# Prompt attention in another order of tiles, its keys and values loaded a stage ahead, and the last row's value pages on two queues

## The reference

```
z = rms_norm(h) @ w_in                      # q, k, v, gates of both groups, 3600 columns
q, k = rms_norm per head half               # 4 heads, two halves of 64 each
prompt:  s_m = q_m k_m^T / 8 + bias(n), causal, m = 0, 1;  p = softmax(s_0) - lam softmax(s_1);  o = p v
sample:  the same against 32 cached pages of each sequence (page_table) and its new tokens
group B: gated linear attention in chunks of 128, prompt and sample
h + concat(rms_norm(o) * gate_d, rms_norm(o_g) * gate_g) @ w_out
```

## Time and profile before

| | us |
|---|---|
| runs: median (lowest, highest) | 1161.14 (1158.05, 1163.96) |
| profiled execution, time | 1162.31 |
| its span | 1160.6 |
| TensorE busy | 1037.6 (89%) |
| VectorE busy | 545.6 (47%) |
| ScalarE busy | 468.1 (40%) |
| GpSimd busy | 234.5 (20%) |
| loads and stores | 200.34 MB, mean 173 GB/s |

### The profile page before, as it was taken

One profiled execution on the slowest core, in us unless ns is written; L12 is line 12 of the kernel. 1 busy time (PEld: TensorE's weight loads), 2 busy tenths in 40 slices (PEclk: granted clock), 3 DMA queues, 4 the chain that ended last, 5 costly groups with the idle time before them and its releaser, 6 DMA issues. The chain is left out here.

```text
span 1160.6 us, 26456 instructions
## 1 busy us (share of the span) xinstructions
PE 1037.6 (89%) x9067; PEld 837.1 (72%) x9067; DVE 545.6 (47%) x1376; ACT 468.1 (40%) x1353; POOL 234.5 (20%) x385
## 2 busy tenths in 40 slices
PE   4999999999999999989899899767686899889978
PEld 4899999977677776656577667546565788778755
DVE  4755533334434332242343434546746766566421
ACT  5732322344443322333323344426646645545330
POOL 0000100013222222120222323339830111011100
PEclk9999999999999999999999999987895799999989
DMA  7322655569898687575799877657223122211101
GB/s 194 121 89 68 203 164 180 147 210 328 288 312 283 228 274 232 191 217 192 246 287 304 306 252 245 209 157 233 72 60 106 49 95 73 73 58 37 54 24 43
DMA packets 111575, 200.34 MB, mean 173 GB/s; under 512 B 15402, under 2 KB 51444, under 8 KB 111444
## 3 DMA queue, kind: packets, MB, share of 16 engines
q1 hardware_dynamic: 75892, 118.22, 33.1%
q0 software_dynamic: 20480, 67.13, 17.1%
q10 hardware_dynamic: 15072, 13.31, 3.4%
HBM read 179.79 MB, written 19.60 MB: 172 GB/s over the span
## 5 line engine op out<-in xcount | busy, mean ns | idle before, releaser
L1149 PE MATMUL bank<-ww,xTh 128*128 128x256 f32 (+1 forms) x1728 | 333.4, 289 | 11.9 <-DVE qwr L1357 9.8
L1149 PEld LDWEIGHTS bank<-ww,xTh 128*128 128x128 f32 (+1 forms) x1728 | 272.6, 188 | 20.4 <-DVE qwr L1357 11.6
L259 POOL DMA_DIRECT2D vraw<-in_cache_v x256 | 138.0, 539 | 622.5 <-issue 620.1
L1149 PE MATMUL bank<-ww,xTl 128*128 128x256 f32 (+1 forms) x864 | 246.0, 285 | 0.0
L477 DVE COPY kt<-bank 128x512 f32<-128x512 f32 x128 | 88.6, 692 | 183.5 <-PE bank L280 119.7
L1149 PEld LDWEIGHTS bank<-ww,xTl 128*128 128x128 f32 (+1 forms) x864 | 162.3, 188 | 0.0
L280 PE MATMUL bank<-ident,kraw 128*128 128x128 f32 x1024 | 153.3, 279 | 0.4 <-DVE kt L477 0.3
L401 ACT ACTIVATE kt<-bank 128x512 f32<-128x512 f32 x128 | 76.2, 595 | 159.6 <-PE bank L280 159.0
L280 PEld LDWEIGHTS bank<-ident,kraw 128*128 128x128 f32 x1024 | 112.8, 141 | 22.5 <-issue 21.6
L302 PE MATMUL bank<-kt,qq 128*32 128x128 f32 x2048 | 81.2, 278 | 17.0 <-DVE kt L477 16.2
L2322 ACT ACTIVATE e<-bank,sm 128x128 f32<-128x128 f32 (+8 forms) x66 | 49.6, 752 | 84.0 <-DVE sm L2433 84.0
(11 more groups left out here) (253 smaller groups left out, 1598.4 us busy)
## 6 DMA issues: line engine op xcount, KB each, us to landing
vraw<-in_cache_v POOLq DMA_DIRECT2D x256, 256.0 KB, 4.6
kraw<-in_cache_k SPq DMA_DIRECT2D x256, 256.0 KB, 4.1
wraw<-in_w_in SPq DMA_DIRECT2D x28, 512.0 KB, 5.2
out<-nat ACTq DMA_DIRECT2D x32, 128.0 KB, 2.0
wo_raw<-in_w_out SPq DMA_DIRECT2D x8, 512.0 KB, 8.8
xr<-in_x_prompt SPq DMA_DIRECT2D x7, 512.0 KB, 3.4
out<-xr SPq DMA_DIRECT2D x7, 512.0 KB, 2.6
bT<-in_x_prompt SPq DMA_DIRECT2D x4, 512.0 KB, 4.2
```

The source lines that it names most:

```text
L259: pool.dma_start(vraw[:, p % VR, :], cache_v.rearrange("a n p h d -> (a n) p (h d)")[bass.ds(page, 1)] .rearrange("o p c -> (o p) c")).the ...
L1149: ins = pe.matmul(z_at(u)[0:r, 0:CB], a[:, k, P * i:P * i + r], b[:, wslot(c), k, :], start=(n == 0), stop=(n == 3 * KT - 1))
```

## The change

The attention stage takes the tiles in the order 3, 7, 6, 5, 4, 2, 1, 0, 8 (order, place); what hung on a tile's number in buffers, semaphores and fills now hangs on its place. Keys are no longer turned one tile ahead: keys 0 to 3 are turned before the first unit, keys 4 to 8 in the first three units of tile 3. For this all key rows are loaded in the linear attention stage, into keys_raw, which lies over w_out's raw blocks 3 to 7; these five blocks are loaded only when the last key is turned, and weights_hi(3) waits for all five. Value rows 0 to 6 are loaded at the end of the linear attention stage, rows 7 and 8 at the start of the attention stage. On ScalarE and VectorE the split of the bias band, and VectorE's wait for the norm weights, stand ahead of the first query and key halves. In the sample attention the odd value pages of the last row are issued by SyncE (by_sp). The meta tokens' rows of the residual are loaded, where a buffer was set to zero before.

```diff
+        KEPT = 3
+        FIRST = 3
+        keys_raw = Area(nc, WOL + 4 * KEPT * D, WOL + 4 * KT * D).take("keys_raw", [P, TILES, W])
+        VD = SB_HIGH - 4 * TILES * W
+        vd = Area(nc, VD, SB_HIGH).take("vd", [P, TILES, W])
...
+        def by_sp(p):
+            return p >= NP - NPAGES and p % 2 == 1
+        def value_in(p):
+            first = NP - NPAGES
+            if by_sp(p):
+                return v_last[p // GRP % 2], 16 * GRP // 2 * ((p - first) // VR + 1)
+            return v_in[p % VR], 16 * (p // VR + 1)
...
+                        if b is not None and t >= 1 and by_sp(b * NPAGES + (t - 1) * GRP + n):
+                            load_value(sp, b * NPAGES + (t - 1) * GRP + n)
...
-                for k in range(KT):
+                for k in range(KEPT):
                     sp.dma_start(wo_raw[:, k, :], w_out[0, k * P:(k + 1) * P, :]).then_inc(wo_in, 16)
...
+                sp.dma_start(first_q[:], q_d[FIRST]).then_inc(first_in, 16)
+                for i in range(TILES):
+                    n = min(P, L - P * i)
+                    sp.dma_start(keys_raw[0:n, i, :],
+                                 k_prompt.rearrange("a b l h d -> (a b l) (h d)")[P * i:P * i + n, :])\
+                      .then_inc(keys_in, 16)
...
+                for i in range(LT_ - 1):
+                    sp.dma_start(vd[:, i, :], v_prompt.rearrange("a b l h d -> (a b l) (h d)")[P * i:P * i + P, :])\
+                      .then_inc(vd_in, 16)
...
-            units = [(i, h) for i in range(TILES - 1) for h in range(H)] + [(TILES - 1, H - 1)]
+            order = [FIRST] + [i for i in range(TILES - 2, -1, -1) if i != FIRST] + [TILES - 1]
+            place = {i: t for t, i in enumerate(order)}
+            units = [(i, h) for i in order[:-1] for h in range(H)] + [(TILES - 1, H - 1)]
...
-                return [[("k", i + 1)], [("q", i + 1, 0)], [("m", i - 1)] if i >= 1 else [], [("q", i + 1, 1)]][h]
+                t, h = place[units[u][0]], units[u][1]
+                x = [[], [("q", order[t + 1], 0)], [("m", order[t - 1])] if t >= 1 else [], [("q", order[t + 1], 1)]][h]
+                if t == 0:
+                    x = x + [[("k", 4), ("k", 5)], [("k", 6)], [("k", 7), ("k", 8)], []][h]
+                return x
+            first_turns = [("q", order[0], 0), ("q", order[0], 1)] + [("k", i) for i in range(FIRST + 1)]
...
+                sp.wait_ge(turned_done, turn_no[("k", TILES - 1)] + 1)
+                sp.wait_ge(wo_in, 16 * KEPT)
+                for k in range(KEPT, KT):
+                    sp.dma_start(wo_raw[:, k, :], w_out[0, k * P:(k + 1) * P, :]).then_inc(wo_in, 16)
...
-                    back = 2 if small(u) else 1
+                    back = 2 if small(u) and small(u - 1) else 1
...
                 def weights_hi(k):
                     if k == 0:
+                        act.wait_ge(wo_in, 16 * KEPT)
+                        act.wait_ge(dw_scaled, 1)
+                    if k == KEPT:
                         act.wait_ge(wo_in, 16 * KT)
-                        act.wait_ge(dw_scaled, 1)
...
-                queries_lo(0, 0)
-                keys_lo(0)
-                queries_lo(0, 1)
                 dve.wait_ge(dw_in, 32)
...
+                for x in first_turns:
+                    if x[0] == "q":
+                        queries_lo(x[1], x[2])
+                    else:
+                        keys_lo(x[1])
```

More of the change, by code:

```diff
@@ L186, in hymba_kernel @@
         v_in = [sem(f"v_in{n}") for n in range(VR)]
-        c_in = sem("c_in")
+        v_last = [sem(f"v_last{n}") for n in range(2)]
         vn_in = sem("vn_in")
@@ L228, in advancer, with load_value @@
             return go
+        def by_sp(p):
[5 more added lines that the diff above has]
+            return v_in[p % VR], 16 * (p // VR + 1)
+        def load_value(eng, p):
+            if p >= VR:
+                b, g = (p - VR) // NPAGES, (p - VR) % NPAGES // GRP
+                eng.wait_ge(pv_done, b * RG + g + 2)
+            page = eng.value_load(pages[0:1, p:p + 1], min_val=0, max_val=POOL - 1)
+            eng.dma_start(vraw[:, p % VR, :],
+                          cache_v.rearrange("a n p h d -> (a n) p (h d)")[bass.ds(page, 1)]
+                          .rearrange("o p c -> (o p) c")).then_inc(value_in(p)[0], 16)
         def decode_sp(sp):
@@ L1880, in hymba_kernel @@
             mix = m_.take("mix_b", [P, W])
+            xr = m_.take("xr", [P, D])
             r4 = m_.take("r4", [P, 3, 4])
@@ L1889, in hymba_kernel @@
             pO = bank[:, 5, :]
-            vd_in = [sem(f"vd_in{n}") for n in range(2)]
             qk_in = [sem(f"qk_in{n}") for n in range(2)]
@@ L1966, in extras @@
                     return []
-                i, h = units[u]
-                return [[("k", i + 1)], [("q", i + 1, 0)], [("m", i - 1)] if i >= 1 else [], [("q", i + 1, 1)]][h]
-            turns = [("q", 0, 0), ("k", 0), ("q", 0, 1)]
+                t, h = place[units[u][0]], units[u][1]
[4 more added lines that the diff above has]
+            first_turns = [("q", order[0], 0), ("q", order[0], 1)] + [("k", i) for i in range(FIRST + 1)]
+            turns = list(first_turns)
             for u in range(NU + 1):
@@ L1990, in wait_bank @@
                     if turns[n][0] == "q":
-                        eng.wait_ge(qlo_done, 2 * turns[n][1] + turns[n][2] + 1)
+                        eng.wait_ge(qlo_done, 2 * place[turns[n][1]] + turns[n][2] + 1)
                     if turns[n][0] == "k":
@@ new lines, in _ @@
+                sp.wait_ge(g_out, 96)
+                load_x(order[0], xr_in)
+                for t in range(1, TILES):
+                    if t >= 2:
+                        sp.wait_ge(mix_done, t - 1)
+                        load_gate(order[t - 1])
+                    if t + 1 < TILES:
+                        if t >= 2:
+                            sp.wait_ge(turned_done, turn_no[("q", order[t - 1], 1)] + 1)
+                        load_q(order[t + 1])
+                    if t >= 3:
+                        store_y(order[t - 3])
+                        sp.wait_ge(y_out, 16 * (t - 2))
+                        load_x(order[t - 2], xr_in)
@@ L2098, in _ @@
+                sp.wait_ge(turned_done, turn_no[("q", order[LT - 1], 1)] + 1)
+                load_x(order[LT], xr8_in)
                 sp.wait_ge(scores_done, 2 * NU)
-                load_x(LT - 1, xr7_in)
+                load_x(order[LT - 1], xr7_in)
                 sp.wait_ge(mix_done, LT)
-                load_gate(LT)
-                for i in range(LT - 2, TILES):
-                    store_y(i)
+                load_gate(order[LT])
+                for t in range(LT - 2, TILES):
+                    store_y(order[t])
@@ L2221, in turn_mix @@
                     r = rows_of(i)
-                    pe.wait_ge(mix_done, i + 1)
+                    pe.wait_ge(mix_done, place[i] + 1)
                     wait_bank(pe, ("m", i))
@@ L2249, in project, with fill @@
                         ins.then_inc(d_free, 1)
-                def fill(u, place):
-                    for i, j in fills.get((u, place), []):
+                def fill(u, at):
+                    for i, j in fills.get((u, at), []):
                         project(i, j)
-                prepare(("q", 0, 0))
-                prepare(("k", 0))
-                prepare(("q", 0, 1))
+                for x in first_turns:
+                    prepare(x)
                 pe.wait_ge(bandhi_done, 2)
@@ L2278, in _ @@
                         scores(u, 1)
-                turn_mix(TILES - 2)
-                for place in range(2):
-                    fill(NU + 1, place)
+                turn_mix(order[-2])
+                for at in range(2):
+                    fill(NU + 1, at)
                 for j in range(8):
-                    project(LT - 1, j)
-                turn_mix(TILES - 1)
+                    project(order[-2], j)
+                turn_mix(order[-1])
                 for j in range(8):
-                    project(LT, j)
+                    project(order[-1], j)
             @block.scalar
@@ L2441, in combine @@
                     dve.wait_ge(exp_done, 2 * u + 2)
-                    if begins(u) and i >= 2:
-                        dve.wait_ge(out_copied, i - 1)
-                    dve.reciprocal(inv[:, i % 2, h:h + 1], s[:, 2:3])
+                    t = place[i]
+                    if begins(u) and t >= 2:
+                        dve.wait_ge(out_copied, t - 1)
+                    dve.reciprocal(inv[:, t % 2, h:h + 1], s[:, 2:3])
                     linked(dve.reciprocal(s[:, 4:5], s[:, 3:4]))
@@ L2511, in projected @@
                 def projected(u):
-                    for i in range(LT - 1):
+                    for i in order[:-2]:
                         if u == first_fill(i) + 4:
```

257 lines of the change are left out of this document (117 added, 140 removed).

## The result

| | before | after |
|---|---|---|
| median, us (13 runs each, same chip) | 1162.23 | 1166.5 |
| lowest to highest, us | 1157.02 to 1163.96 | 1161.8 to 1173.25 |
| profiled execution, us (its span) | 1162.31 (1160.6) | 1166.45 (1164.8) |

The ratio of after to before is 1.0047, with a 95% interval of 1.0033 to 1.0061. So the kernel is slower by 4 to 7 us of 1162. The forecast was 1165.0, in a range of 1155 to 1178. The difference is real by its interval and just inside the 0.5% that the prediction called "the same". Two parts of opposite sign hide in it, which the experiments take apart: about -5 us for the pages and +10 for attention. Experiments 4, 5 and 8 had one execution each far outside the others (1670.82, 1303.11 and 1668.13 us, at a mean granted clock of 0.557, 0.759 and 0.557), which the ratios leave out.

A forecast was written before the change was run, and what follows sets the result against it. It took page issue to bound the last row, a chain across engines attention's half-clock start, and TensorE the rest. Terms -5.0 + 9.2 + 10.0 - 3.6 - 3.8 - 3.0 = +3.8 us gave 1165, range 1155 to 1178.

The forecast's parts named there:

- the same: Whole kernel: a time within 0.5% (5.8 us) of before, between 1155.3 and 1166.9 us; chance 0.45.
- Last row's pages: Sample attention: issuing the last row's value pages from two queues removes TensorE's waits; -5.0 us, range -3.0 to -7.8.
- The last wait: Last row, sign of being right: TensorE has no wait for value pages but the last, under 2 us.
- Start of the stage: Attention start: norm weights' wait and four key turns instead of one delay the first exponential; +9.2 us, bounds +7 and +11.
- Tile 3: First tile's four units, with key turns and weights, take 35.9 us instead of 25.9; +10.0 us, bounds +5 and +14.
- The new wait on the weights of row 3: Tile 3's third unit: ScalarE stands 4.3 us for five late loads, so that step is 12.0 us instead of 7.7.
- Tile 7: Without projections, three units of 6.9 us, one of 8.6 and 1.5 for half clock; -3.6 us, bounds -5 and 0.
- Rival 1: Slower: half clock reaches through tile 7, 11 us in three units less the 1.5 counted; 1174 us, chance 0.22.
- Keys: Tiles 6, 5, 4 and 2 no longer turn keys: 1.6, 1.6, 0.3 and 0.3 us less; -3.8 us, bounds -5 and -2.
- Tiles 1 and 0: With projections, TensorE sets their pace at 20.0 and 17.1 us, and the end behind is the same work; -3.0 us.
- 2 (faster, 1155): Tile 3's units overlap better, its block 29 us, and the first key turns go in 6 instead of 8.5; chance 0.15.
- 3 (the queue does nothing): Last row: transfers and not issue bound the value pages, so the second queue gains nothing; +5, 1170 us, chance 0.11.

The follow-up runs named there:

- experiment 4: Changed kernel with a semaphore for each of the five late weight loads, so ScalarE waits for row 3 alone: 1163.32 against 1161.08 us, ratio 1.0019.
- experiment 5: Changed kernel with VectorE's wait for norm weights and the scaling moved behind the first low halves: 1162.19 against 1160.59 us, ratio 1.0007.
- Experiment 8: Changed kernel with the edits of experiment 4 and experiment 5, plus ScalarE's query copy ahead of the exponential in tile 7: 1157.86 us, ratio 0.9983.
- experiment 2: Changed kernel with all value pages issued by GpSimd again, so the attention part alone: 1171.09 against 1161.08 us, ratio 1.0083.
- experiment 1: Kernel before with only the last row's odd value pages issued by SyncE: 1156.03 against 1161.08 us, ratio 0.9953.
- experiment 7: The kernel of experiment 4 with filler matmuls on TensorE in tile 3 and tile 7's first three units: 1159.13 against 1160.59 us, ratio 0.9986.
- Experiment 3: Changed kernel with tile 3 first, then upward 0, 1, 2, 4 to 7: 1167.78 against 1161.08 us, ratio 1.0052.
- experiment 10: Changed kernel with tiles 1 to 7, then 0, all weight rows loaded ahead, experiment 5's edit, keys turned a tile ahead: 1154.57 us, ratio 0.9951.
- experiment 9: Changed kernel with the edits of experiment 4 and experiment 5, plus eight 128-column filler matmuls behind each first turn: 1164.24 us, ratio 1.002.

## Why the forecast came out right, point by point

**Last row's pages.** The mechanism was right, and the size was right by the experiments: 5.1 us alone, 4.2 by the ratios of experiment 2 and the changed kernel (1.0083 and 1.0047). In the traces I measured the stretch from one and the same late issue of a value page (719.19 us before, 715.15 after) to the begin of attention. It is 5.0 to 5.7 us shorter than before in eight of the ten experiments with this edit; 4.4 and 9.0 in the two others (in the second the linear attention stage was itself nearly 2 us shorter), and 2.8 in the changed kernel, which had a wait of 1.64 us where most others had 0.3 to 0.8. In experiment 2, without the edit, it is 0.5 us shorter. That this execution was 4.0 us ahead already at that issue is not shown to be the edit's: executions with the edit stood there from 4.0 us ahead to 0.2 behind, the one of experiment 2, without it, 0.4 ahead, and already at the first issue of a value page (251.73 us before) they differ by 2.5 us ahead to 1.9 behind. The last wait was to be the only one and under 2 us; it is 1.8 to 2.6, and one more, of 0.3 to 1.6, stands ahead of it.

A rule of the Trainium skill ("DMA: Bandwidth & Descriptors", Issuing engines are not separate DMA queues) spoke against this part. It says that more issuing engines save issue time alone; here issue time was what was short, so experiments 1 and 2 agree with it.

**Start of the stage.** Forecast +9.2, trace +9.6, and the way there was right: scores were to start 8.5 us later after the stage's begin (883.3 against 874.79) and start 8.7 later (16.2 us behind it against 7.5). What the forecast did not split, experiment 5 does: 2.5 us of the price are VectorE's wait for the norm weights and only the rest is keys.

**Tile 3.** The four steps were forecast as 8.8, 7.7, 12.0 and 7.4 us and are 8.6, 8.1, 13.2 and 6.7. The new wait on the weights of row 3 is there, ended by the load, 6.1 instead of 4.3 us; in three other traces with the same wait it is 4.6 to 5.1, so part of its excess here is this execution's. Experiment 4 gives up to 4.4 us back and with it shows what the forecast didn't say: the wait is for the fifth load, while the first lands in 4.1 us. Without the wait the third unit was forecast as 7.7 us; it is 9.6 in experiment 4 and 7.4 in experiment 7, where it has the whole clock. So of the other 6.3 us some 2.3 are half clock, which the forecast's list of steps left out; the rest is key turns and weights by that list, and no run took these out.

**Tile 7.** This step failed, -1.9 instead of -3.6: "three units of 6.9". The first is 6.90, but the second is 9.04 and the third 7.92 us, and the 1.5 us set aside for half clock in the first did not come: its granted clock was 1.00. These rows of the changed kernel, from the timelines of PE, ACT and DVE, show why:

```profile
920.82 0.60 PE L2254 MATMUL bank<-ident,qd 128*128 128x128 f32 x4
...
925.19 1.09 PE L2219 MATMUL bank<-ident,e 128*128 128x128 f32 x4 [3.33 <-DVE qs L2521]
```

```profile
921.62 1.13 ACT L2415 ACTIVATE woh<-wo_raw,wsc 128x1024 fp32r<-128x1024 f32 x1
...
923.74 0.58 ACT L2339 ACTIVATE qs<-bank 128x512 fp32r<-128x512 f32 x1
```

```profile
924.35 0.69 DVE L2521 TENSOR_TENSOR qs<-bank,qs 128x512 fp32r<-128x512 f32 x1 [1.72 <-ACT qs L2339]
```

The turned query lay in its bank from 921.4 on; ScalarE came to it at 923.74, behind a weight and an exponential; only after VectorE's half was the bank free for the second batch of probabilities. In the third unit the turn of the mixed heads holds the same bank, for 1.82 us. The forecast's chain left out these copies and the weight, which still falls in tile 7's units. Experiment 8 gives 1.2 us of the tile back.

Half clock in this tile was rival 1's reason and one of the forecast's signs of being wrong. By windows over the four units the granted clock was 1.00, 0.81, 1.00 and 1.00. The 0.81 follows the wait of 3.33 us: from 925.19 to 928.99 the clock was 0.55. The same 16 matmuls of values took 3.16 us there and 2.01 in the next unit:

```profile
926.07 3.16 PE L2237 MATMUL bank<-vd,pT_b 128*128 128x128 f32 x16
```

So about 1 us of the second unit's excess is half clock, if this work was on its chain, which no run shows: experiment 7's filler left the clock of this unit at 0.82. Rival 1 is right in kind and far too large in size; the low clock came behind one long wait and did not reach through the tile.

**Keys, and tiles 1 and 0.** Keys: -4.3 for -3.8. Tiles 1 and 0 together with the end: -3.2 for -3.0, but in another place. Tile 1 was right (20.0); tile 0's units took 4.5 us where the forecast comes to 4.3, its step to the last tile took 8.4 beyond a unit where tile 7's took 6.7, and the end, which was to be "the same work", is 2.8 us shorter. Experiment 3 ends with tile 7 and has 57.6 us there, experiment 10 with tile 0 and has 54.6: what stands next to last decides it. It isn't the same work, since the last unit of that tile is transposed and multiplied by values behind the last tile's first exponential, ahead of its second scores. TensorE's values there, before (tile 7) and after (tile 0):

```profile
1105.47 1.95 PE L2199 MATMUL bank<-vd,pT_b 128*128 128x128 f32 x16
...
1111.72 0.38 PE L2237 MATMUL bank<-vd,pT_b 128*128 128x128 f32 x2
```

The last tile's second exponential comes 10.9 us behind its first (1110.13 to 1120.99) and came 13.2 behind before (1103.12 to 1116.30), which is 2.3 of the 2.8 us.

**The rivals.** 1 (half clock, 1174): the clock over tile 7's four units was 0.95, and what it is shown to cost lies in tile 3. 2 (faster, 1155): the loads did not land in time as the kernel waits for them, and the start did not go faster. 3 (the queue does nothing): excluded by experiments 1 and 2. That the total is within 2 us of the forecast owes something to luck: tile 7 came out 1.7 us and tiles 1 and 0 2.6 us above their terms, the end 2.8 and the pages 1.9 us below.

## What to carry to other kernels

Price a change of order at its seams: the start of the stage with its first tile, where no engine is full, cost 20 us here, while the order behind it was worth 3. A semaphore that counts several loads makes the first user wait for the last of them; where the loads are issued late, one for each gave 3 to 4.4 us for no work. When two edits of opposite sign come together, run each alone before you judge either: the pages alone gained 5 us that the whole change hid.

## What the runs showed of the hardware

TensorE's clock stayed at 0.50, the lower of its two levels, in the start of experiment 9 though the records have TensorE busy from 856.7 to 872 us with hardly a gap, while three fillers of 512 columns at a time raised it from 0.72 to 1.00 in the third unit of tile 3. The matmuls of the start were 128 columns each, with a weight load for each, and eight of them took 1.74 us (862.60 to the next turn at 864.34). The Trainium skill ("TensorE: Matmul & The Clock Gate", Part 1: The HAM clock gate) has activity release the throttle; in experiment 9 a TensorE that is busy by its records did not release it, and no run here tells why.

The second queue's pages landed no later than GpSimd's, though the forecast's bound was 2 us later. Over the whole execution the medians from issue to landing are 3.5 us for SyncE's 16 pages and 4.8 for GpSimd's 240, but SyncE's are all from the last row, when no other loads run. In that stretch alone (715 to 757 us) they are near each other:

```profile
vraw<-in_cache_v POOLq DMA_DIRECT2D x15, 256.0 KB, 3.9
vraw<-in_cache_v SPq DMA_DIRECT2D x14, 256.0 KB, 3.4
```

In the same stretch of experiment 1 both are 3.9, so no run shows a difference between the queues.
